# Attention output kept as features: halves added by GpSimd, output bank copied by ScalarE and VectorE in turn

## The reference: what is computed

```python
def block_attention(q, k, v, scale):          # per head, over 128-query blocks
    sc = jnp.einsum('bqkgd,bskd->bkgqs', qblk, k) * scale
    p = jax.nn.softmax(sc, axis=-1)
    return jnp.einsum('bkgqs,bskd->bqkgd', p, v)
...
    oa = block_attention(qa, ka, va, ...)      # 8 query heads, 2 key heads, value width 64
    ob = block_attention(qm, km, vb, ...)      # 8 latent heads, value width 64
    o = concatenate([rms_norm(oa, p['out_norm_a']), rms_norm(ob, p['out_norm_b'])])
    x = x + einsum('bse,ed->bsd', o, p['w_o'])
    h2 = rms_norm(x, p['norm_ffn'])
    x = x + expert_choice_moe(h2, w_router, w_gate, w_up, w_down)   # 16 experts, 64 tokens each and set
```

## Time and profile before

| | us |
|---|---|
| median of 3 executions (1082.73 to 1084.68) | 1083.67 |
| profiled execution, device time | 1086.1 |
| its span, first to last instruction | 1083.7 |
| TensorE busy | 1044.8 |
| VectorE busy | 886.0 |
| ScalarE busy | 775.3 |
| GpSimd busy | 423.3 |

### The profile page before, as it was taken

One profiled execution on the slowest core, in us unless ns is written; L12 is line 12 of the kernel. 1 busy time (PEld: TensorE's weight loads), 2 busy tenths in 40 slices (PEclk: granted clock), 3 DMA queues, 4 the chain that ended last, 5 costly groups with the idle time before them and its releaser, 6 DMA issues.

```text
span 1083.7 us, 16970 instructions
## 1 busy us (share of the span) xinstructions
PE 1044.8 (96%) x5689; PEld 896.7 (83%) x5689; DVE 886.0 (82%) x1147; ACT 775.3 (72%) x1095; POOL 423.3 (39%) x394
## 2 busy tenths in 40 slices
PE   8999999999999999998699999999999999999995
PEld 7999978999889987887578888888888888888884
DVE  6787669989999843338899999999999999999991
ACT  7655569888998843344577877877878878788771
POOL 2466576111358502334524432344323444234101
PEclk9999999999999999999799999999999999999998
DMA  8232050010211348741799999999999999999982
GB/s 305 79 116 102 1 197 1 2 41 20 98 41 40 98 109 263 225 164 79 235 417 378 398 400 400 400 421 400 401 400 400 413 408 401 400 400 406 415 310 39
DMA packets 77936, 266.05 MB, mean 245 GB/s; under 512 B 11249, under 2 KB 13516, under 8 KB 77628
## 3 DMA queue, kind: packets, MB, share of 16 engines
q1 hardware_dynamic: 69776, 239.68, 56.9%
q0 software_dynamic: 8048, 25.68, 8.3%
q10 hardware_dynamic: 60, 0.01, 0.0%
HBM read 239.07 MB, written 26.28 MB: 245 GB/s over the span
## 4 chain that ended last, share of the span: by engine, by line
PE 48%; DVE 2%; DMA 1%; issue 1%; ACT 0%; POOLq 0%; POOL 0%; DVEq 0%; ACTq 0%
PE ps L2003 10%; PE ps L2005 10%; PE ps L2004 10%; PE ps L2017 5%; PE ps L2019 5%; PE ps L2018 5%; PE ps L1980 1%; DMA xe<-h,idxT 1%; DMA out<-y,give 1%; DVE lo L2171 0%; DVE idx L1776 0%; DVE affT L1785 0%; DVE gates L1771 0%; ACT hi L2093 0%; POOLq L2274 0%
## 5 line engine op out<-in xcount | busy, mean ns | idle before, releaser
L2171 DVE TENSOR_TENSOR lo<-raw,hi 128x2048 fp32r<-128x2048 f32 x191 | 430.0, 2285 | 32.3 <-ACT hi L2093 32.0
L2093 ACT ACTIVATE hi<-raw 128x2048 fp32r<-128x2048 f32 x192 | 364.6, 1918 | 70.0 <-PE ps L2005 57.3
L2003 PE MATMUL ps<-hi,xehi 128*128 128x512 f32 x480 | 188.3, 392 | 1.3 <-DVE h L2193 1.0
L2005 PE MATMUL ps<-hi,xelo 128*128 128x512 f32 x480 | 186.9, 389 | 0.0
L2004 PE MATMUL ps<-lo,xehi 128*128 128x512 f32 x480 | 186.8, 389 | 0.0
L1939 POOL DMA_INDIRECT xe<-h,take x60 | 111.1, 1851 | 25.1 <-issue 13.7
L2003 PEld LDWEIGHTS ps<-hi,xehi 128*128 128x128 f32 x480 | 90.1, 188 | 20.2 <-issue 1.4
L2005 PEld LDWEIGHTS ps<-hi,xelo 128*128 128x128 f32 x480 | 90.1, 188 | 18.8
L2004 PEld LDWEIGHTS ps<-lo,xehi 128*128 128x128 f32 x480 | 90.2, 188 | 18.1
L1934 POOL COPY take<-idx 128x4 uint32 (+1 forms) x15 | 29.0, 1930 | 193.7 <-DVE xt L2187 187.4
L1361 DVE TENSOR_TENSOR probTlo<-ps,probThi 128x512 fp32r<-128x512 f32 x128 | 87.8, 686 | 12.1 <-ACT probThi L1318 10.0
(11 more groups left out here) (302 smaller groups left out, 2192.3 us busy)
## 6 DMA issues: line engine op xcount, KB each, us to landing
...
```

Source lines behind the costliest of these rows:

```text
L2003: pe.matmul(ps[:, dst[n], :], rowhi[:, c, :], hi[w][:, cols], start=c == 0, stop=False)
L2005: last = pe.matmul(ps[:, dst[n], :], rowlo[:, c, :], hi[w][:, cols], start=False, stop=c == KD - 1)
L2093: act.activation(hi[s][:], raw[s][:], ACT.Copy).then_inc(hi_done, 1)
L2171: dve.tensor_tensor(lo[s][:], raw[s][:], hi[s][:].bitcast(F32), ALU.subtract).then_inc(lo_done, 1)
```

## The change

The output is never turned into rows. It stays features by tokens:

- The bank of even heads is copied by ScalarE and that of odd heads by VectorE, at the same step 4g + 9, into one of two buffers. From the third head on the copy waits until GpSimd has added the halves of head g - 2.
- SyncE moves rows 64 to 127 of the copy down to rows 0 to 63 of a ring of three (`move_half`, 128 KB). GpSimd adds rows 0 to 63 to them (`add_halves`), in its program two heads later. SyncE stores the sum (`store_head`) before it goes on to the next head's move.
- The sums of exponentials are turned once a set (`turn_reciprocals`), after the reciprocal, and stored. `load_rows` loads them for a tile, broadcast over the features, and VectorE multiplies (`normalise`).
- `turn_output`, `halves` and `o_transposes` go. The high and low parts of a tile's output are taken from SBUF. The sums of squares are made from the squares (ScalarE) by two additions on GpSimd (`group_sums`) and a product with a column of ones (`group_squares`), and `group_means` takes them out of the bank.
- The tiles' output has two buffers in place of three, and `load_rows` waits accordingly. SyncE asks for the first tile's rows behind head 28 and for the second's behind head 29. The splits of output weights are at other heads. The loop has 6 steps behind the last unit in place of 8.

The core of the diff:

```diff
-    o_dram = nc.dram_tensor("attention_out", [T * P, D], F32).ap()
-    o_rows = o_dram.rearrange("(t p) d -> t p d", p=P)
+    o_dram = nc.dram_tensor("attention_out", [T, P, KD, P], F32).ap()
+    r_dram = nc.dram_tensor("reciprocal_sums", [SETS, TS, 2, KD, P], F32).ap()
...
-        att["ot"] = bm("ot", [P, SEQ])
+        att["ot"] = [bm(f"ot{i}", [P, SEQ]) for i in range(2)]
+        att["sums"] = [pj[0:VD, :, C_CQ + r * P:C_CQ + (r + 1) * P] for r in range(OUT_RING)]
...
-        def store_heads(s, h0, h1):
-            cols = slice(h0 * VD, h1 * VD)
-            sp.wait_ge(o_done, HEADS * s + h1)
-            sp.dma_start(o_rows[TS * s:TS * (s + 1), :, cols].rearrange("t p d -> p t d"),
-                         att["rows"][s][0][:, :, cols]).then_inc(o_stored, 16)
-
-        for h0, h1 in O_PARTS:
-            store_heads(0, h0, h1)
-        sp.wait_ge(o_stored, 16 * len(O_PARTS))
-        for i in range(KD // 2):
+        def move_half(g):
+            sp.wait_ge(ot_copied, g + 1)
+            if g >= OUT_RING:
+                sp.wait_ge(o_stored[g % OUT_RING], STORED + 16 * (g // OUT_RING))
+            sp.dma_start(att["sums"][g % OUT_RING], att["ot"][g % 2][VD:P, :].rearrange("d (i t) -> d i t", i=TS)).then_inc(
+                ot_moved[g % 2], 16)
+
+        def store_head(g):
+            s, h = g // HEADS, g % HEADS
+            sp.wait_ge(o_added, g + 1)
+            sp.dma_start(o_dram[TS * s:TS * (s + 1), h % 2 * VD:(h % 2 + 1) * VD, h // 2, :].rearrange("i p t -> p i t"),
+                         att["sums"][g % OUT_RING]).then_inc(o_stored[g % OUT_RING], 16)
+
+        def store_reciprocals(s):
+            sp.wait_ge(r_copied, s + 1)
+            sp.dma_start(r_dram[s].rearrange("i e c t -> (i e c) t"), att["rsumT"][:, s, :]).then_inc(r_stored, 16)
+
+        def load_output_weights(i):
             if i >= 2:
                 sp.wait_ge(wo_lo, 2 * (i - 1))
+            if i == 3:
+                sp.wait_ge(wo_loaded, 16 * 3)
             sp.dma_start(wo["raw"][:, 2 * (i % 2):2 * (i % 2) + 2, :],
                          a["w_o"].rearrange("(k p) n -> p k n", p=P)[:, 2 * i:2 * i + 2, :]).then_inc(wo_loaded, 16)
-        route_first(sp)
-        for h0, h1 in O_PARTS[:-1]:
-            store_heads(1, h0, h1)
-        route_second(sp)
-        store_heads(1, *O_PARTS[-1])
+
+        for g in range(ALL):
+            move_half(g)
+            store_head(g)
+            if g == HEADS - 1:
+                load_output_weights(0)
+                load_output_weights(1)
+                store_reciprocals(0)
+            elif g == HEADS + 3:
+                load_output_weights(2)
+            elif g == HEADS + 6:
+                load_output_weights(3)
+            elif g == ALL - 4:
+                route_first(sp, g + 1)
+            elif g == ALL - 3:
+                route_second(sp)
+        store_reciprocals(1)
         route_rest(sp)
...
+        def add_halves(g):
+
+            lower = att["sums"][g % OUT_RING]
+            pool.wait_ge(ot_moved[g % 2], MOVED + 16 * (g // 2 + 1))
+            pool.tensor_tensor(lower, lower, att["ot"][g % 2][0:VD, :].rearrange("d (i t) -> d i t", i=TS), ALU.add).then_inc(o_added, 1)
...
-            pool.wait_ge(wo_loaded, 16 * (KD // 2) if i >= KD - 4 else 16 * 2)
+            pool.wait_ge(wo_loaded, 16 * (2 if i < 4 else i // 2 + 1))
...
+        split_at = {HEADS + 2: 0, HEADS + 3: 1, HEADS + 4: 2, HEADS + 6: 3, HEADS + QH: 4, HEADS + QH + 1: 5,
+                    HEADS + QH + 3: 6, HEADS + QH + 4: 7}
...
+        for g in range(GROUP, ALL):
+            if g in keys[2:]:
+                split_values(g)
             if g in copies:
...
+                copy_rotary_keys(g)
+            if g in split_at:
+                split_output_weights(pool, split_at[g])
+            add_halves(g - 2)
+        add_halves(ALL - 2)
+        group_sums(0)
+        add_halves(ALL - 1)
...
-        def turn_output(g, i):
...
-            dst, cols = ps[:, O_BANK, i * VD:(i + 1) * VD], slice(i * P, (i + 1) * P)
-            turned = pe.matmul(dst, ot[:, cols], k["halves"][:], start=True, stop=True)
-            if i == TS - 1:
-                turned.then_inc(o_ready, 1)
+        def turn_reciprocals(s):
+            pe.wait_ge(rsum_done, s + 1)
+            pe.transpose(ps[0:HEADS * TS, R_BANK, s * P:(s + 1) * P],
+                         att["sum"][:, s * HEADS * TS:(s + 1) * HEADS * TS], k["ident"][:]).then_inc(r_turned, 1)
...
-            output = (u - 11) // TS if u >= 11 and (u - 11) % TS == 0 else None
-            for i in range(TS):
-                if output is not None:
-                    turn_output(output, i)
-                if turned is not None:
+            if turned is not None:
+                for i in range(TS):
                     transpose_prob(turned, i)
             if pair is not None:
                 values(pair)
-            if u == NU - 3:
-                o_transposes(0, 0)
-            elif u == NU:
-                o_transposes(0, 1)
-            elif u == NU + 3:
+            if u in (HALF + 4, NU + 2):
+                turn_reciprocals(u // HALF - 1)
+            if u == NU + 3:
                 product(0, 0)
                 product(0, 1)
             elif u == NU + 4:
                 product(0, 2)
-                o_transposes(1, 0)
                 product(0, 3)
...
-            if u >= 9 and (u - 9) % TS == 0:
+            if u >= 9 and (u - 9) % (2 * TS) == 0:
                 g = (u - 9) // TS
                 act.wait_ge(pv_done, TS // 2 * (g + 1))
-                if g:
-                    act.wait_ge(o_ready, g)
-                act.activation(ot[:], ps[:, OT_BANK, :], ACT.Copy).then_inc(ot_copied, 1)
+                if g >= 2:
+                    act.wait_ge(o_added, g - 1)
+                    act.wait_ge(ot_copied, g)
+                act.activation(ot[g % 2][:], ps[:, OT_BANK, :], ACT.Copy).then_inc(ot_copied, 1)
...
+            if u >= 9 + TS and (u - 9) % (2 * TS) == TS:
+                g = (u - 9) // TS
+                dve.wait_ge(pv_done, TS // 2 * (g + 1))
+                if g >= 2:
+                    dve.wait_ge(o_added, g - 1)
+                dve.wait_ge(ot_copied, g)
+                dve.tensor_copy(ot[g % 2][:], ps[:, OT_BANK, :]).then_inc(ot_copied, 1)
...
-            if u >= 11 and (u - 11) % TS == 0:
-                g = (u - 11) // TS
-                h = g % HEADS
...
+            if u in (HALF + 2, NU + 1):
+                s = u // HALF - 1
+                sums = att["sum"][:, s * HEADS * TS:(s + 1) * HEADS * TS]
+                dve.wait_ge(exp_done, HALF * (s + 1))
+                dve.reciprocal(sums, sums).then_inc(rsum_done, 1)
+            elif u in (HALF + 6, NU + 4):
+                s = u // HALF - 1
+                dve.wait_ge(r_turned, s + 1)
+                dve.tensor_copy(att["rsumT"][:, s, :], ps[0:HEADS * TS, R_BANK, s * P:(s + 1) * P]).then_inc(r_copied, 1)
...
+            if u == NU - 3:
+                normalise(0, 0)
+            elif u == NU - 1:
                 o_low(0, 0)
+            elif u == NU:
+                normalise(0, 1)
...
+        t = ORDER[j]
+        if j >= 2:
+            sp.wait_ge(otlo_done, 2 * (j - 1))
+            sp.wait_ge(osq_done, j - 1)
+            sp.wait_ge(o_ready, 2 * j)
+        sp.dma_start(o[j % 2][:], o_dram[t]).then_inc(o_loaded[j % 2], 16)
+        for half in range(2):
+            sp.dma_start(r[min(j, 1)][half * VD:(half + 1) * VD], r_dram[t // TS, t % TS, half].partition_broadcast(VD)).then_inc(
+                r_loaded[min(j, 1)], 16)
+        if j >= 3:
+            sp.wait_ge(x1_done, 2 * (j - 2))
+        sp.dma_start(xr[j % 3][:], x_dram[t]).then_inc(xr_loaded[j % 3], 16)
+
+    def wait_for_stores(sp, heads, sets):
+        for i in range(OUT_RING):
+            sp.wait_ge(o_stored[i], STORED + 16 * len(range(i, heads, OUT_RING)))
+        sp.wait_ge(r_stored, STORED + 16 * sets)
+
+    def sync_first(sp, heads):
         sp.wait_ge(wo_lo, KD)
+        wait_for_stores(sp, heads, 1)
...
+        def group_sums(j):
+            squares = osq[:].rearrange("p (g c) t -> p g c t", g=2)
+            pool.wait_ge(osq_done, j + 1)
+            steps.did(pool.tensor_tensor(squares[:, :, 0:2, :], squares[:, :, 0:2, :], squares[:, :, 2:4, :], ALU.add))
+            steps.wait()
+            if j:
+                pool.wait_ge(ss_ready, j)
+            pool.tensor_tensor(acc[:], squares[:, :, 0, :], squares[:, :, 1, :], ALU.add).then_inc(acc_done, 1)
+
+        def group_root(j):
+            pool.wait_ge(sso_done, j + 1)
+            pool.tensor_tensor(ro(j), sso(j), k["minus_half"][:, 0:2], ALU.pow).then_inc(ro_done, 1)
...
+        def group_squares(j):
+            pe.wait_ge(acc_done, j + 1)
+            if j == 0:
                 pe.wait_ge(prep_lo, preps)
...
+                pe.wait_ge(ones_ready, 1)
+            for n in range(2):
```

(28 more changed lines are left out.)

262 lines of the change are left out of this document (126 added, 136 removed).

## The result

The changed kernel takes 1102.95 us (median of 4 executions, 1101.79 to 1105.62), the kernel before 1083.26 (4, 1082.73 to 1084.68) on the same chip. The ratio is 1.0183, with an interval of 1.0162 to 1.0204. The forecast was 1068 with a range of 1060 to 1082: the sign was wrong, and the time lies outside the range. The profiled execution took 1101.79 us, with a span of 1099.9.

A forecast was written before the change was run, and what follows sets the result against it. TensorE, busy 96% of the span, was taken as the bound, with VectorE close behind in grouped-query heads. Terms: 11.2 + 6.4 + 3.1 + 2.0 - 3.3 - 2.0 - 1.6 = 15.8 us off, median 1068, range 1060 to 1082.

The forecast's parts named there:

- (a): Attention, 16 latent heads: each loses the 0.70 us turn of its output on TensorE, 11.2 us off.
- (b): Attention, 16 grouped-query heads: VectorE and ScalarE lose work, each head 0.4 us shorter, 6.4 us off; ends 0 and 11.2.
- (e): Attention, GpSimd: adds behind splits of output weights delay output copies after head 15, 3.3 us lost; ends 0 and 8.
- (c): Output projection: 16 blocks of four transposes go, sums of squares and two transposes of sums come, net 3.1 us off.
- (d): Output projection, late rows of tile 2: the wait and its low-clock loss shrink, 2.0 us saved; ends 0 and 3.8.
- (f): End of attention, SyncE: first rows of the next stage come late, VectorE stands 3.0 us, 2.0 lost; ends 0 and 5.
- (g): Clock: one of the waits in (e) and (f) brings TensorE's lower clock, 1.6 us lost; ends 0 and 3.2.
- The experts' stage is untouched: Experts, the last stage: unchanged in length, it only starts 15.8 us earlier.
- R1: Slower: SyncE's serial move, add and store bound a head from a 5.6 us move; at 6 us, 1097 us; chance 0.08.
- R2: Slower: in output-projection tiles the sums-of-squares chain ends after TensorE asks, costing 17 us, 1085 us; chance 0.05.
- R3: Little gain: (e), (f) and (g) at their far ends, 9.3 us more, 1077; with (b) at 0, 1083; chance 0.14.
- R4: Attention not shortened: VectorE's and ScalarE's mutual waits leave half of (a), none of (b); 12 us less gain, 1080; chance 0.07.

The follow-up runs named there:

- The last kernel: Changed kernel with wide `ones`, moves and gains by ScalarE, first rows behind head 26, first four splits a head later, gains and router weights behind head 30: 1075.87 us.
- The short splits: Changed kernel with wide `ones`, GpSimd's split of output weights cut from 6.4 to 2.4 us, gain and true low part left out: 1082.01 us, ratio 0.9968.
- five kernels: Changed kernel with all tiles, or only expert-weight buffers, at old place: 1095.15, 1095.09 us; kernel before shifted by 320, 128, 64 bytes: 1092.64, 1091.78, 1093.0 us.

## Why the prediction was wrong, step by step

At the choice of tokens the forecast was off by 15.8 + 10.0 = 25.8 us, and the experts added 6.2. By stretches of the table:

- **(a) latent heads: right, a little large.** 7.2 us a head, predicted 7.1. Two latent heads took 15.57 us and now take 14.45: 0.56 saved each, not 0.70, so 9.0 us, not 11.2. The last kernel, with its waits removed, keeps 8.1 at the end of attention for (a) and (b) together.
- **(b) grouped-query heads: failed, 0 and not 6.4.** The lower bound was the truth. The prediction read VectorE at 28.4 of 30 us and still counted 0.4 us of shortening a head. VectorE loses 0.61 a head and gains 0.60 every second head, yet from head 0's copy to head 5's the time went from 34.63 to 34.25 us, 0.08 a head, and its busy share is 96%. In the last kernel, without the waits of (e), the lead over the kernel before is 4.5 us at head 15's copy and 4.4 at head 20's: again nothing, though there ScalarE also makes gain products between the two. The short splits put nothing on another engine: their lead goes from 4.9 to 5.6 us, 0.14 a head. VectorE and ScalarE wait for each other there (the 0.35 us at 193.36 is one such wait), and I priced the two engines' sums instead of that order. That this is the whole reason is argued; no run took VectorE's work away.
- **(c) output projection: right for a tile, the sum a little large.** Each step from logits to logits, tile by tile from the second on: 14.57, 14.76, 14.78 and 13.18 us before, 14.16, 14.31, 14.34 and 12.79 after, so 0.39 to 0.45 shorter, predicted 0.45. The last two steps gained nothing.
- **(d) the stall at the third tile: failed, wrong sign.** Predicted an idle of 1.1 us and 2.0 saved. Measured: from the first logits to the second 22.25 us after and 14.62 before, 7.6 lost. The path from the last head's copy to the landed rows took 420.30 - 396.31 = 24.0 us where about 17 was worked out. The prediction had 5 us for the loads; they took 420.30 - 411.26 = 9.0. Even in the kernel before this tile's rows took 6.8 (401.52 to 408.36), and after, 4 MB of expert weights are asked for close behind them (from 413.80); how much of the 9.0 is due to those was not separated. The other 3 come mainly from the last head's move, issued at 400.92 in place of 397.0, because the move before it stood behind the second tile's rows.
- **(e) GpSimd: mechanism and heads right, size too small.** The waits came at heads 18, 19 and 20 (1.06, 1.32, 2.35) where 0, 1.3 and 2.5 were worked out. That they agree so closely is partly luck, since both sides of the race came later than worked out: the first split began 14.0 us after head 15's copy and not 11.1, and head 18's copy was due at 20.7 and not 18.8. From the copy of head 15 to that of head 20 the time went from 33.8 to 38.1 us, 4.3 lost, predicted 3.3. What was missed: the add takes 1.28 us, not 1.05 as the 128x512 product took the earlier trace rows; and "from head 21 on it holds" was wrong. Splits 4 to 7 repeat it (0.42 us at head 25, 1.44 at 28, 1.23 at the second latent keys). Above all, the backlog was not carried into (f). The short splits, 13 us, show the price of the whole.
- **(f) SyncE: mechanism right, size wrong, 9.0 and not 2.0.** The rows were predicted 11.3 us after head 28's copy starts and came 17.6 after (385.28 - 367.69). Of the 6.3 more, 4.4 are the move of head 28, issued at 372.74 and not 368.3, since SyncE still serves head 27; the rest is mainly the loads with their broadcast sums, 6.2 us (379.04 to 385.28) in place of the 4 I gave them. And TensorE has no "one and a half units" to run on: of VectorE's 9.52 us it lost 8.96. The far end, 5, was too near.
- **(g) clock: too small.** Predicted 1.6; the two stretches shown give 4.1.
- **The range.** Its better ends add up to 11.2 + 9 + 3.1 + 3.8 - 1.5 - 0.5 = 25.1 us, not 24, so its lower end would be 1058.6. That changes nothing here.
- **"The experts' stage is untouched": failed.** It was argued from the program. The stage's instructions were unchanged and its buffers were not: 7 to 9 us, shown by five kernels. Against the kernel before it shows as 6.2, as the changed kernel's stage at the old addresses is some 1 to 1.5 us shorter.
- **Hidden:** the move took 2.4 us in the median, as assumed, so the one size that I called unmeasured was right, and the store 2.4. But a move right behind rows takes 5.9 to 7.3 us (381.28 to 387.15, 391.58 to 398.91). The sums of squares in a tile did not stop TensorE in undisturbed tiles, as forecast; they did where the rows were late, and also for 1.88 us in the first.

**The rivals.** R1's place was right and its price wrong: it named the serial chain move, add, store, move, and asked for a move above 5.6 us. At 2.4 the chain is hidden in a steady state, but it keeps SyncE a head behind after every split and puts the rows behind that. Moves issued elsewhere gave 8.6 us. R2 did not occur by itself. R3, the far ends of (e), (f) and (g), was nearest in kind: the three came together, because they are one chain. They were priced apart, as independent terms with ends of their own; a backlog on GpSimd delays adds, adds delay SyncE, and SyncE delays rows. R4 was right for (b) and wrong for (a).

The contention rule quoted in the prediction shows in the changed kernel itself. Timeline of a tile of the output projection, after.

```profile
441.81 1.29 POOL L1563 TENSOR_TENSOR osq<-osq 128x512 f32<-128x512 f32 x1 [4.84 <-ACT osq L1725]
442.44 1.21 DVE L1799 TENSOR_TENSOR otlo<-o,othi 128x512 fp32r<-128x512 f32 x1
443.18 1.07 POOL L1567 TENSOR_TENSOR acc<-osq 128x256 f32<-128x256 f32 x1
```

VectorE's low half has two SBUF inputs. It lasts 1.21 us, where its line takes 0.69 with no GpSimd instruction beside it, and ends 0.55 us after GpSimd's addition has ended. GpSimd's next addition lasts 1.07 us, where it takes 0.74 alone (498.77). The same pattern stands in five tiles, with 0.91 to 1.21 us for VectorE. The Trainium skill's rule ("SBUF — State Buffer", "Who interferes with whom") agrees with these rows: each engine holds the other up. The prediction had GpSimd alone held up, by 0.7 us; it was 0.33. TensorE did not wait for the sums in four of the five tiles; in the fifth, at 428.12, the rows were late.
